# The input loaded and squared in halves of a row block, and two norms' roots made by row block

## The chip, the cores and the metric

The kernel runs on one core of one Trainium2 chip. The metric is the time of one execution on the device in microseconds (us). Three runs of the kernel before gave 892.39, 893.02 and 893.70 us; the median is 893.02 us. In what follows PE is TensorE (the matrix engine), PEld its weight loads, ACT is ScalarE, DVE is VectorE, POOL is GpSimd and SP is SyncE, which here only issues DMA transfers.

## The reference

Two transformer blocks follow each other on 256 rows of 1024 numbers. The first thing that is computed, and what the change touches, is the norm ahead of the first matrix product; the same norm stands ahead of the cross attention:

```python
def rmsnorm(x, g):
    xf = x.astype(jnp.float32)
    y = xf * lax.rsqrt(jnp.mean(xf * xf, axis=-1, keepdims=True) + EPS)
    return (y * g.astype(jnp.float32)).astype(x.dtype)

def first_block(x, mem, ...):
    h = rmsnorm(x, pre_mix_g[l])
    aq, ak, av, hq, hf_fwd, hf_bwd, hi, hg = split_columns(h @ w_in[l], IN_SPLITS)
    ...                                   # self attention and a gated recurrence, joined in `mixed`
    x = x + rmsnorm(mixed, post_mix_g[l])
    h = rmsnorm(x, pre_x_g[l])
    m = rmsnorm(mem, mem_norm_g[l])
    x = x + rmsnorm(memory_cross_attention(h, m, ...), post_x_g[l])
    h = rmsnorm(x, pre_ffn_g[l])
    x = x + rmsnorm(conv_ffn(h, ...), post_ffn_g[l])
```

The second block has the same skeleton: a norm, a large product `h @ w_in`, two kinds of attention, a projection, a norm and a feed-forward net.

## The kernel before

The 256 rows are two row blocks (R = 2) of 128 rows, one row to a partition; `x[:, r, :]` is row block r. Every engine has a program of its own, written out in order, and the engines meet only at semaphores.

**Weights.** SP loads the weights in transfers of mostly 1 MB or less into a ring of four halves. What lies there is cut into pieces of 128x1024 numbers, and each is split in two: ACT writes the rounded high part (`sb_whi`, line 1631), DVE the rest (`sb_wlo`, line 2266), and PE multiplies high by high, high by low and low by high. ACT can only write a high part when the piece that lay in its place has been used by PE, and SP can only load into a half when DVE is done with what lay there. `ahead_of(name, n)` in the program of ACT or DVE marks up to which piece the engine works before it goes on.

**The first norm** (`pre_mix_g`) in the order of its steps:

- SP issues one transfer of 512 KB for each row block of x (line 1473), then the first weight piece (line 1450) and the rest (line 1452).
- ACT squares a whole row block, 128x1024, and the instruction sums along the row (line 1647); a short instruction behind it reads the sum out.
- POOL makes the inverse root from the sum: one TENSOR_SCALAR (mean plus epsilon, line 1501), a wait on its own step, and a power of -0.5 (line 1502).
- DVE multiplies the row block by the root, in two halves of 512 columns (line 2278). It has all four of these ahead of the low part of the first weight piece (line 2266) and that ahead of the low parts of the turned tiles (line 2288).
- PE turns the scaled rows (line 776) into eight tiles of 128 columns by 256 rows. ACT writes the tiles' high parts (line 1662), after the high part of the first weight piece (line 1631); DVE writes their low parts. PE's first product (line 578) needs both.

Ahead of all that PE multiplies zeros (line 766). POOL issues two small transfers behind the second root (lines 1529 and 1531).

**The norm of the cross attention** (`pre_x_g`): ACT squares x in halves of a row block as DVE adds them up (line 1653), four sums in all. POOL waits for all four, adds two and two (line 1511), and makes both row blocks' roots in one go (lines 1501 and 1502). DVE then scales row block 0 (line 2278) and ACT row block 1 (line 1974). PE turns them (line 754) when all four halves are scaled, behind the last product of the fourth part of the memory's weights (`xkv3`). Two of the banks that the turned tiles go to hold that product's results until ACT has copied them out (line 1710).

**`rstd_rows`** (line 1514) is the helper that later norms use: for one row block it takes the first sum as it comes, folds the second in with another TENSOR_SCALAR (lines 1519 and 1521), and makes the root (line 1522).

Of the kernel before, what the change touches and what calls it, by code (L numbers as in the profile page):

```python
# [33 lines left out]
ACT = mybir.ActivationFunctionType  # L34
# [121 lines left out]
def build(nc, a, out):  # L156
    ctx = ExitStack()
    with ctx:
# [132 lines left out]
        for n in GAINS:  # L291
            stats[n] = (stat(R if n in ("pre_mix_g", "mem_norm_g") else 2 * R), stat(R))
        for n in ("w_out", "w_xo", "ffn1", "w_o_2", "ffn2"):
# [49 lines left out]
        def gain_at(name):  # L343
            return COL_GAIN + KT * GAINS.index(name)
# [1095 lines left out]
        def _(sp):  # L1440
# [31 lines left out]
            for r in range(R):  # L1472
                sp.dma_start(x[:, r, :], a["x"][r * P:(r + 1) * P, :]).then_inc(s(f"x_in{r}"), 16)
            load_all(names[:SLOTS])
# [13 lines left out]
        def _(pool):  # L1488
# [37 lines left out]
            for r in range(R):  # L1526
                sums, rstds = (t[:, r:r + 1] for t in stats["pre_mix_g"])
                rstd("pre_mix_g", [(s("pre_mix_g_sq"), r + 1)], sums, D, rstds)
            pool.dma_start(posi[:, :], a["positions_2"].rearrange("(r p) -> p r", p=P),
# [23 lines left out]
            rstd_post("w_out")  # L1553
            rstd_post("pre_x_g")
            for r in range(R):
# [47 lines left out]
        def _(act):  # L1603
# [33 lines left out]
            def pre_norm(name, src, waits, T, gain, between, added=None, before=None):  # L1637
# [5 lines left out]
                for r in range(R):  # L1643
                    if not added:
                        for w in waits[r]:
# [30 lines left out]

            pre_norm("pre_mix_g", x, [[(s(f"x_in{r}"), 16)] for r in range(R)], hT1, gain_at("pre_mix_g"), first_tiles)
            ahead_of("hff", 4)
# [290 lines left out]
            def between_x():  # L1969
                ahead_of("w_xq0", 1)  # L1970
                act.wait_ge(s("pre_x_g_rstd"), 1)
                for c in range(2):
                    q = slice(c * 512, (c + 1) * 512)
                    act.activation(rows[:, 1, q], x[:, 1, q], ACT.Copy, scale=stats["pre_x_g"][1][:, 1:2]
                                   ).then_inc(s("pre_x_g_scaled"), 1)
                ahead_of("w_xq0", 2)
                for r in range(R):
                    take_rows(f"xkv3.{r}", xv[:, r, 512:1024])
# [257 lines left out]
        def _(dve):  # L2236
# [35 lines left out]
            def pre_norm(name, src, T, gain, before, between):  # L2272
                before()
                for r in range(1 if name == "pre_x_g" else R):
                    dve.wait_ge(s(f"{name}_rstd"), r + 1 if name == "pre_mix_g" else 1)
                    for c in range(2):
# [817 lines left out]
```

## Time and profile before

| what | value |
|---|---|
| median of three runs | 893.02 us (892.39 to 893.70) |
| the profiled execution's own time | 893.71 us |
| its span, first to last instruction | 891.9 us |
| PE busy | 880.6 us, 99% of the span |
| DVE busy | 647.9 us, 73% |
| ACT busy | 493.8 us, 55% |
| POOL busy | 92.8 us, 10% |
| DMA, mean over the span | 171 GB/s |
| mean granted PE clock | 0.998 of full speed |

The profiled execution was timed by itself at 893.71 us, 1.8 us more than the span that the profile shows. Busy time says how full an engine was; it doesn't say who waited for whom. For that the page has the chain of work that ended last: 92% of it is PE's.

### The profile page before, as it was taken

The page shows a single profiled execution, that of the slowest core. Times are in us where ns is not written, and L with a number is a line of the kernel's source. Part 1 is how long each engine was busy: PE and PEld are TensorE (multiplying, and loading weights), DVE is VectorE, ACT ScalarE, POOL GpSimd, SP SyncE. Part 2 cuts the span into 40 slices and gives each one's busy share as a digit, 9 for nine tenths or more (in the row PEclk, how much of TensorE's full clock was granted, in tenths as well). Part 3 has the DMA queues.
Part 4 walks back from the last instruction along what each step waited for, and adds up shares of the span by engine and source line. Part 5 has one row for each costly group of instructions (what it writes and reads, how often), then busy time and mean ns, then how long its engine had stood idle before and what let it go on. Part 6 is the DMA issues. An engine that isn't in the chain of part 4 may idle for free.

```text
span 891.9 us, 13262 instructions
## 1 busy us (share of the span) xinstructions
PE 880.6 (99%) x5100; PEld 754.1 (85%) x5100; DVE 647.9 (73%) x1024; ACT 493.8 (55%) x880; POOL 92.8 (10%) x123
## 2 busy tenths in 40 slices
PE   8999999999999999999999999999999999999997
PEld 6988997889889888888789887898888888888886
DVE  5789975574879688789856846677687774766774
ACT  5855665474477465566635366676555772324341
POOL 1324100010010000000133300011031100000000
PEclk9999999999999999999999999999999999999999
DMA  9745423453654455556418644344266554564531
GB/s 314 248 155 177 163 97 131 153 193 115 189 200 154 142 175 185 208 181 245 166 60 283 211 143 142 107 161 170 95 229 195 169 186 142 189 212 165 189 142 48
DMA packets 99502, 152.25 MB, mean 171 GB/s; under 512 B 2608, under 2 KB 66352, under 8 KB 99184
## 3 DMA queue, kind: packets, MB, share of 16 engines
q1 hardware_dynamic: 99040, 150.68, 50.3%
q8 instruction: 41, 0.67, 0.3%
q10 hardware_dynamic: 288, 0.47, 0.2%
q0 software_dynamic: 112, 0.26, 0.1%
q14 instruction: 21, 0.17, 0.1%
HBM read 150.35 MB, written 1.05 MB: 170 GB/s over the span
## 4 chain that ended last, share of the span: by engine, by line
PE 92%; DVE 5%; ACT 2%; issue 1%; DMA 1%; POOL 0%; DVEq 0%; POOLq 0%; SPq 0%; ACTq 0%
PE ps L578 28%; PE ps L571 19%; PE ps L1080 13%; PE ps L636 8%; PE ps L1084 7%; PE ps L668 4%; PE ps L743 2%; PE ps L754 1%; PE ps L831 1%; DVE sb_wlo L2266 1%; PE ps L707 1%; PE ps L1028 1%; PE ps L932 1%; PE ps L1224 1%; ACT sb_whi L1631 1%
## 5 line engine op out<-in xcount | busy, mean ns | idle before, releaser
L2266 DVE TENSOR_TENSOR sb_wlo<-sb_ring,sb_whi 128x1024 fp32r<-128x1024 f32 (+2 forms) x169 | 203.5, 1215 | 81.6 <-ACT sb_whi L1631 81.1
L1631 ACT ACTIVATE sb_whi<-sb_ring 128x1024 fp32r<-128x1024 f32 (+2 forms) x169 | 174.0, 1046 | 101.5 <-PE ps L636 69.5
L578 PE MATMUL ps<-sb_whi,sb_tb 128*128 128x512 f32 (+2 forms) x520 | 128.8, 387 | 0.0
L578 PEld LDWEIGHTS ps<-sb_whi,sb_tb 128*128 128x128 f32 x520 | 93.9, 188 | 17.3 <-issue 1.0
L578 PE MATMUL ps<-sb_whi,sb_ta 128*128 128x512 f32 (+1 forms) x240 | 57.8, 380 | 0.0
L636 PE MATMUL ps<-sb_wlo,sb_tb 128*128 128x512 f32 (+2 forms) x224 | 57.7, 380 | 0.0
L1519 POOL TENSOR_SCALAR sb_st<-sb_st 128x1 f32<-128x1 f32 x14 | 7.3, 524 | 451.6 <-ACT sb_probs L1895 451.6
L2224 ACT ACTIVATE sb_b<-sb_b 128x512 f32<-128x512 f32 x9 | 5.7, 632 | 79.7 <-DVE sb_b L2695 79.7
L578 PEld LDWEIGHTS ps<-sb_whi,sb_ta 128*128 128x128 f32 x240 | 42.3, 188 | 8.6 <-issue 0.5
L636 PEld LDWEIGHTS ps<-sb_wlo,sb_tb 128*128 128x128 f32 x224 | 41.3, 188 | 7.6
L2695 DVE TENSOR_REDUCE sb_b<-ps 128x256 f32<-128x512 f32 x36 | 23.8, 685 | 28.6 <-PE ps L1084 28.6
L1998 ACT ACTIVATE sb_b<-ps 128x256 f32<-128x256 f32 x32 | 12.2, 382 | 52.7 <-PE ps L1084 52.7
L571 PE MATMUL ps<-sb_whi,sb_ta 128*128 128x512 f32 (+1 forms) x120 | 37.5, 377 | 0.1
L578 PE MATMUL ps<-sb_tb,sb_whi 128*128 128x256 f32 x256 | 35.1, 288 | 0.8 <-DVE sb_tb L2288 0.7
L578 PEld LDWEIGHTS ps<-sb_tb,sb_whi 128*128 128x128 f32 x256 | 32.1, 191 | 2.6 <-issue 1.6
L1710 ACT ACTIVATE sb_b<-ps 128x512 f32<-128x512 f32 (+1 forms) x44 | 24.2, 590 | 9.6 <-PE ps L743 4.6
L578 PE MATMUL ps<-sb_ta,sb_whi 128*128 128x256 f32 x192 | 26.5, 290 | 1.4 <-DVE sb_ta L2288 1.4
L2266 DVE TENSOR_TENSOR lent9lo<-sb_ring,lent9hi 128x1024 fp32r<-128x1024 f32 x19 | 23.2, 1220 | 5.9 <-ACT lent9hi L1631 5.9
L2266 DVE TENSOR_TENSOR lent1lo<-sb_ring,lent1hi 128x1024 fp32r<-128x1024 f32 x18 | 22.0, 1221 | 7.5 <-ACT lent1hi L1631 7.5
L2755 DVE SCALAR_TENSOR_TENSOR sb_b<-sb_b,sb_col 128x255 f32<-128x255 f32 x64 | 26.6, 478 | 0.8 <-ACT sb_b L2016 0.8
L578 PEld LDWEIGHTS ps<-sb_ta,sb_whi 128*128 128x128 f32 x192 | 24.8, 197 | 2.0 <-issue 1.6
L571 PEld LDWEIGHTS ps<-sb_whi,sb_ta 128*128 128x128 f32 x120 | 21.9, 188 | 4.7 <-DVE sb_ta L2714 0.5
(430 smaller groups left out, 2068.0 us busy)
## 6 DMA issues: line engine op xcount, KB each, us to landing
sb_ring<-in_w_in SPq DMA_DIRECT2D x32, 1024.0 KB, 5.4
sb_ring<-in_w_up SPq DMA_DIRECT2D x18, 1024.0 KB, 5.1
sb_ring<-in_w_down SPq DMA_DIRECT2D x11, 1024.0 KB, 7.4
sb_ring<-in_w_ffn_down SPq DMA_DIRECT2D x11, 1024.0 KB, 7.5
sb_ring<-in_w_ffn_gate SPq DMA_DIRECT2D x9, 1024.0 KB, 5.3
sb_ring<-in_w_ffn_up SPq DMA_DIRECT2D x9, 1024.0 KB, 5.4
sb_ring<-in_w_xkv SPq DMA_DIRECT2D x8, 1024.0 KB, 5.6
sb_ring<-in_w_out SPq DMA_DIRECT2D x4, 1024.0 KB, 5.1
```

Source lines behind the costliest of these rows:

```text
L571: mm = pe.matmul(o, l[a_], r[b_], start=(start and n == 0), stop=(stop and n == 2), skip_group_check=not check)
L578: pe.matmul(o, l, r, start=(start and n == 0), stop=False, skip_group_check=True)
L636: mm = pe.matmul(o, T[0][:, k0 + i, r * P:(r + 1) * P], w[1][:, i], start=False, stop=k0 + i == k - 1, skip_group_check=True)
L668: mm = pe.matmul(o, T[0][:, k0 + i, r * P:(r + 1) * P], w[1][:, i], start=False, stop=k0 + i == k - 1, skip_group_check=True)
L743: mm = pe.matmul(o, w[1][:, i, :], T[0][:, i, :], start=False, stop=i == KT - 1, skip_group_check=True)
L1080: pe.matmul(o[:, :], w[0][:, k, :], both_halves[f][:, k].rearrange("p two n -> p (two n)"), start=k == 0, stop=False)
L1084: mm = pe.matmul(o[:, 0:S], w[1][:, k, :], T[0][:, k, :], start=False, stop=k == KT - 1)
L1631: act.activation(piece_pair(m)[0], src, ACT.Copy).then_inc(s("hi_done"), 1)
L1710: act.activation(dst, bank[banks.at[key][0]][:, 0:n], ACT.Copy, scale=1.0 if scale is None else scale).then_inc(banks.release(key), 1)
L2266: dve.tensor_tensor(low, pieces[m][1], high.bitcast(F32), ALU.subtract).then_inc(s("lo_done"), 1)
L2695: dve.tensor_reduce(dst[c], o[:, :].rearrange("p (two n) -> p n two", two=2), AX.X, ALU.add).then_inc(banks.release(key), 1)
L2755: dve.scalar_tensor_tensor(dst, src, COL[:, at:at + 1], dst, ALU.mult, ALU.add).then_inc(banks.release(key) if last and c and i < SPLIT_FR ...
```

## The change

The input comes in four transfers of 128x512 in place of two of 128x1024, each with a semaphore of its own. ACT squares it in four halves, each with a sum of its own. Both norms' roots are made by `rstd_rows`, one row block at a time. DVE and ACT wait for the count of the roots that they need: DVE's scaling of row block r waits for root r, and in the cross attention ACT, which scales row block 1, waits for two.

```diff
@@ stats
-            stats[n] = (stat(R if n in ("pre_mix_g", "mem_norm_g") else 2 * R), stat(R))
+            stats[n] = (stat(R if n == "mem_norm_g" else 2 * R), stat(R))
@@ SP
             for r in range(R):
-                sp.dma_start(x[:, r, :], a["x"][r * P:(r + 1) * P, :]).then_inc(s(f"x_in{r}"), 16)
+                for c in range(2):
+                    q = slice(c * 512, (c + 1) * 512)
+                    sp.dma_start(x[:, r, q], a["x"][r * P:(r + 1) * P, q]).then_inc(s(f"x_in{r}{c}"), 16)
@@ POOL
             for r in range(R):
-                sums, rstds = (t[:, r:r + 1] for t in stats["pre_mix_g"])
-                rstd("pre_mix_g", [(s("pre_mix_g_sq"), r + 1)], sums, D, rstds)
+                rstd_rows("pre_mix_g", r)
@@
-            rstd_post("pre_x_g")
+            for r in range(R):
+                rstd_rows("pre_x_g", r)
@@ ACT
                 for r in range(R):
-                    if not added:
+                    if name == "pre_mix_g":
+                        for c in range(2):
+                            act.wait_ge(s(f"x_in{r}{c}"), 16)
+                            q = slice(c * 512, (c + 1) * 512)
+                            act.activation(rows[:, r, q], src[:, r, q], ACT.Square,
+                                           accum_out=stats[name][0][:, 2 * c + r:2 * c + r + 1]
+                                           ).then_inc(s(f"{name}_sq"), 1)
+                    elif not added:
...
-            pre_norm("pre_mix_g", x, [[(s(f"x_in{r}"), 16)] for r in range(R)], hT1, gain_at("pre_mix_g"), first_tiles)
+            pre_norm("pre_mix_g", x, [], hT1, gain_at("pre_mix_g"), first_tiles)
@@
-                act.wait_ge(s("pre_x_g_rstd"), 1)
+                act.wait_ge(s("pre_x_g_rstd"), R)
@@ DVE
-                    dve.wait_ge(s(f"{name}_rstd"), r + 1 if name == "pre_mix_g" else 1)
+                    dve.wait_ge(s(f"{name}_rstd"), 1 if name == "mem_norm_g" else r + 1)
```

POOL at the start of the program, ahead of its first two transfers. `sb_st` holds sums and roots, `sb_neghalf` the power. Before:

```order
L1525 MEMSET sb_neghalf 128x32
L1501 ISA
L1501 TENSOR_SCALAR sb_st<-sb_st 128x1 [waits pre_mix_g_sq,pool_step]
L1502 TENSOR_TENSOR sb_st<-sb_st,sb_neghalf 128x1 [waits pool_step]
L1501 TENSOR_SCALAR sb_st<-sb_st 128x1 [waits pre_mix_g_sq]
L1502 TENSOR_TENSOR sb_st<-sb_st,sb_neghalf 128x1 [waits pool_step]
```

Now:

```order
L1527 MEMSET sb_neghalf 128x32
L1521 ISA
L1521 TENSOR_SCALAR sb_st<-sb_st 128x1 [waits pre_mix_g_sq,pool_step]
L1523 TENSOR_SCALAR sb_st<-sb_st 128x1 [waits pre_mix_g_sq,pool_step]
L1524 TENSOR_TENSOR sb_st<-sb_st,sb_neghalf 128x1 [waits pool_step]
L1521 TENSOR_SCALAR sb_st<-sb_st 128x1 [waits pre_mix_g_sq]
L1523 TENSOR_SCALAR sb_st<-sb_st 128x1 [waits pre_mix_g_sq,pool_step]
L1524 TENSOR_TENSOR sb_st<-sb_st,sb_neghalf 128x1 [waits pool_step]
```

Each row block's root has three instructions in place of two, and the first of them waits only for the first half's sum. The two transfers stand behind six instructions in place of four.

ACT at the start of the program, from its first transfer to the first tile's high part (`sb_ta`). `sb_b` is where the squares go. Before:

```order
L1605 DMA sb_col<-in_ident_col 128x374
L1647 ACT_TABLE_LOAD
L1647 ACTIVATE sb_b0,sb_st<-sb_x 128x1024 [waits x_in0]
L1647 ACTIVATE sb_b0,sb_st<-sb_x 128x1024 [waits x_in1]
L1673 DMA sb_cst<-in_tables 128x544
L1631 ACTIVATE sb_whi<-sb_ring 128x1024 [waits first_piece_in]
L1662 ACTIVATE sb_ta<-ps4,sb_col 128x256 [waits filled4,col_in]
```

Now:

```order
L1607 DMA sb_col<-in_ident_col 128x374
L1650 ACT_TABLE_LOAD
L1650 ACTIVATE sb_b0,sb_st<-sb_x 128x512 [waits x_in00]
L1650 ACTIVATE sb_b0,sb_st<-sb_x 128x512 [waits x_in01]
L1650 ACTIVATE sb_b0,sb_st<-sb_x 128x512 [waits x_in10]
L1650 ACTIVATE sb_b0,sb_st<-sb_x 128x512 [waits x_in11]
L1682 DMA sb_cst<-in_tables 128x544
L1633 ACTIVATE sb_whi<-sb_ring 128x1024 [waits first_piece_in]
L1671 ACTIVATE sb_ta<-ps4,sb_col 128x256 [waits filled4,col_in]
```

Two squares of 128x1024 have become four of 128x512, each with a wait on its own transfer. The high part of the first weight piece still stands behind all squares and ahead of the tiles.

POOL between the norm behind the self attention (`w_out_sq`) and the one ahead of the feed-forward net, in the first block. Before:

```order
L1511 TENSOR_TENSOR sb_st<-sb_st 128x2 [waits w_out_sq]
L1501 TENSOR_SCALAR sb_st<-sb_st 128x2 [waits pool_step]
L1502 TENSOR_TENSOR sb_st<-sb_st,sb_neghalf 128x2 [waits pool_step]
L1511 TENSOR_TENSOR sb_st<-sb_st 128x2 [waits pre_x_g_sq]
L1501 TENSOR_SCALAR sb_st<-sb_st 128x2 [waits pool_step]
L1502 TENSOR_TENSOR sb_st<-sb_st,sb_neghalf 128x2 [waits pool_step]
L1519 TENSOR_SCALAR sb_st<-sb_st 128x1 [waits w_xo_sq]
```

Now:

```order
L1513 TENSOR_TENSOR sb_st<-sb_st 128x2 [waits w_out_sq]
L1503 TENSOR_SCALAR sb_st<-sb_st 128x2 [waits pool_step]
L1504 TENSOR_TENSOR sb_st<-sb_st,sb_neghalf 128x2 [waits pool_step]
L1521 TENSOR_SCALAR sb_st<-sb_st 128x1 [waits pre_x_g_sq]
L1523 TENSOR_SCALAR sb_st<-sb_st 128x1 [waits pre_x_g_sq,pool_step]
L1524 TENSOR_TENSOR sb_st<-sb_st,sb_neghalf 128x1 [waits pool_step]
L1521 TENSOR_SCALAR sb_st<-sb_st 128x1 [waits pre_x_g_sq]
L1523 TENSOR_SCALAR sb_st<-sb_st 128x1 [waits pre_x_g_sq,pool_step]
L1524 TENSOR_TENSOR sb_st<-sb_st,sb_neghalf 128x1 [waits pool_step]
```

In place of one addition, one mean and one power for both row blocks there are two rounds of mean, mean and power, the first of which needs only row block 0.

## Rows read from the trace of the kernel before

**Rows 1.** What PE waited for in the span: in total, times, longest.

```profile
PE ps L578 <- DVE sb_ta L2288: 1.4, 1, 1.4
...
PE ps L578 <- DVE sb_tb L2288: 0.7, 1, 0.7
...
PE ps L754 <- DVE sb_b L2278: 0.2, 1, 0.2
```

**Rows 2.** Timeline of ACT, 0 to 15 us: start, length, what, idle before.

```profile
5.21 1.06 ACT L1647 ACTIVATE sb_b<-sb_x 128x1024 f32<-128x1024 f32 x1 [2.76 <-DMA sb_x<-in_x]
...
6.59 1.06 ACT L1647 ACTIVATE sb_b<-sb_x 128x1024 f32<-128x1024 f32 x1 [0.23 <-DMA sb_x<-in_x]
...
7.55 0.19 ACT L1647 ACTIVATION_READ_ACCUMULATOR sb_b<-sb_x 128x1 f32 x1
8.34 1.06 ACT L1631 ACTIVATE sb_whi<-sb_ring 128x1024 fp32r<-128x1024 f32 x1 [0.60 <-DMA sb_ring<-in_w_in]
```

**Rows 3.** Timeline of POOL, 0 to 12 us.

```profile
6.53 0.19 POOL L1501 TENSOR_SCALAR sb_st<-sb_st 128x1 f32<-128x1 f32 x1 [5.68 <-ACT sb_b L1647]
6.80 0.55 POOL L1502 TENSOR_TENSOR sb_st<-sb_st,sb_neghalf 128x1 f32<-128x1 f32 x1
7.83 0.49 POOL L1501 TENSOR_SCALAR sb_st<-sb_st 128x1 f32<-128x1 f32 x1 [0.47 <-ACT sb_b L1647]
8.40 0.55 POOL L1502 TENSOR_TENSOR sb_st<-sb_st,sb_neghalf 128x1 f32<-128x1 f32 x1
```

**Rows 4.** Timeline of DVE, 0 to 15 us.

```profile
7.39 0.88 DVE L2278 TENSOR_SCALAR sb_b<-sb_x,sb_st 128x512 f32<-128x512 f32 x2 [1.58 <-POOL sb_st L1502]
8.98 1.09 DVE L2278 TENSOR_SCALAR sb_b<-sb_x,sb_st 128x512 f32<-128x512 f32 x2 [0.71 <-POOL sb_st L1502]
9.99 1.21 DVE L2266 TENSOR_TENSOR sb_wlo<-sb_ring,sb_whi 128x1024 fp32r<-128x1024 f32 x1
11.12 3.21 DVE L2288 SCALAR_TENSOR_TENSOR sb_ta<-ps,sb_col,sb_ta 128x256 fp32r<-128x256 f32 x8
```

**Rows 5.** Timeline of PE, 0 to 18 us.

```profile
12.13 3.52 PE L578 MATMUL ps<-sb_ta,sb_whi 128*128 128x256 f32 x16 [1.35 <-DVE sb_ta L2288]
```

**Rows 6.** Timeline of ACT, 181 to 189 us, around the second norm.

```profile
182.98 0.63 ACT L1653 ACTIVATE sb_b<-sb_x 128x512 f32<-128x512 f32 x1
183.51 0.19 ACT L1653 ACTIVATION_READ_ACCUMULATOR sb_b<-sb_x 128x1 f32 x1
...
185.88 1.34 ACT L1974 ACTIVATE sb_b<-sb_x,sb_st 128x512 f32<-128x512 f32 x2 [0.57 <-POOL sb_st L1502]
187.13 1.04 ACT L1631 ACTIVATE sb_whi<-sb_ring 128x1024 fp32r<-128x1024 f32 x1
188.20 1.09 ACT L1710 ACTIVATE sb_b<-ps 128x512 f32<-128x512 f32 x2
```

**Rows 7.** The chain of waits, 165 to 215 us: start, length, what.

```profile
187.71 0.47 PE ps L636 x2
```

**Rows 8.** POOL's second mean of a row block (line 1521), all 14.

```profile
L1521 POOL TENSOR_SCALAR sb_st<-sb_st x14: 264/265/1640, 242.8 to 887.1; 128x1 f32<-128x1 f32 x14
```

**Rows 9.** Timeline of SP, 0 to 16 us: DMA issues, and their length.

```profile
0.73 0.86 SPq L1473 DMA_DIRECT2D sb_x<-in_x  x2
...
2.10 8.02 SPq L1452 DMA_DIRECT2D sb_ring<-in_w_in  x4
```

**Rows 10.** Busy time of engines by stretch, granted clock, DMA share, GB/s.

```profile
4.00:6.50 2.50, 2.50 (x4) 1.01 (x3) 0.41 (x3) 1.15 (x2) 0.00 (x0) 1.00 1.03 380
6.50:8.50 2.00, 1.46 (x8) 0.83 (x7) 0.88 (x2) 1.31 (x3) 1.33 (x4) 1.00 1.19 309
```

**Rows 11.** The same view, of the stretch at the lower clock.

```profile
13.67:17.09 3.42, 3.42 (x16) 3.42 (x17) 2.93 (x4) 1.31 (x2) 0.00 (x0) 0.50 1.08 342
```

**Rows 12.** The chain of waits, 0 to 40 us.

```profile
17.39 1.07 ACT sb_whi L1631
...
35.98 1.60 DVE sb_b L2278 x4
```

## Prediction

> **What bounds the kernel now.** I read four views, in this order. First, what PE waited for. PE is busy for 99% of the span, so a change pays only where PE stands still. Three of its stops lie where this change could touch them: 1.4 us ahead of its first product, 0.2 us ahead of the memory's turned rows, 0.7 us behind the cross attention's norm [rows 1]. Second, the start engine by engine. The first product begins at 12.13 us [rows 5]. Read back from there: DVE's low parts of the tiles from 11.12, its low part of the first weight piece from 9.99, its scaling of row block 1 from 8.98 [rows 4]; POOL's power from 8.40 and mean from 7.83 [rows 3]; ACT's square of row block 1 from 6.59, which had waited for x [rows 2]. Every step begins within 0.1 us of the last one's end, so this chain has no slack. Beside it runs one with little: the first weight piece is there at 8.34 and its high part is done at 9.40 [rows 2], 0.59 us before DVE begins its low part. Third, the second norm: ACT scales row block 1 from 185.88, writes a high part from 187.13, and copies `xkv3` out from 188.20 [rows 6]; PE ends the half of `xkv3` that the copy waits for at 187.71 + 0.47 = 188.18 [rows 7]. So PE sets that start, and the root does not. Fourth, the granted clock: from 13.67 to 17.09 us PE ran at 0.50, its lower level of 1.2 GHz, and at 1.00 around it [rows 11]. It had stood still for 1.35 us ahead of the first product [rows 5]. At 2.4 GHz the 3.42 us of work would have taken 1.71.
>
> **The change part by part.**
>
> *Squares.* Two of 1.06 us become four. For a half I take the second norm's squares: read-out begins 183.51 - 182.98 = 0.53 us after the start and takes 0.19 [rows 6], so the sum is there after 0.72 us, against 7.55 + 0.19 - 6.59 = 1.15 [rows 2]. Only the last half counts: 0.43 us gained if it lands when the row block landed. The first half of each block is squared while the second lands; ACT was idle there (2.76 us).
>
> *Transfers.* The bytes are the same; the source rows are 2 KB long in place of 4 KB, and SP issues two more transfers at 0.86 / 2 = 0.43 us each [rows 9]. So the first weight piece is issued 0.86 us later. From above: the next four issues took 8.02 us [rows 9], 2.0 us each against 0.43, so SP was held up by a full queue and the engines by nothing; the DMA share was already 1.03 [rows 10]. A later issue into a queue that isn't empty costs nothing; at the worst it costs the 0.86 us whole. The Trainium skill speaks for the full queue (DMA: Bandwidth & Descriptors, "Queues, rings and completion order": each engine takes its ring's descriptors in order), so by it the weight piece simply stays behind x. For the shorter rows the trace has no pure case. The nearest are 380 GB/s with x's 4 KB rows and 309 with the weight piece's 512 B rows [rows 10]. 1.05 MB takes 2.76 us at the one and 3.39 at the other: between 0 and 0.63 us later. Rows of 2 KB are nearer to the long ones; I take 0.2 us later for x's halves and for the weight piece. Lower end: the weight piece no longer competes with x, which may land up to 0.2 us earlier.
>
> *POOL.* Row block 0: first half seen early, second half at 5.21 + 0.2 = 5.41, its sum at 6.13. Then a start of 0.09 (as 7.74 to 7.83), a second mean of 0.265 [rows 8], 0.08 to the next, a power of 0.55 [rows 3]: root at 7.11, DVE from 7.15, 0.24 earlier than 7.39. Row block 1: last sum at 6.59 + 0.2 + 0.72 = 7.51. Its two means would begin at 7.17 and 7.60. Here a row speaks against the change: POOL's mean took 0.49 us at 7.83 and 0.19 at 6.53 [rows 3]; the long one began inside DVE's scaling (7.39 to 8.27) and ended 0.05 us behind it [rows 4]. Both means of row block 1 now fall into DVE's scaling of row block 0 (7.15 to 8.03). With the long price: first mean to 7.66, second 7.74 to 8.08, power to 8.71, DVE from 8.74. Without: second mean to 7.87, power to 8.50, DVE from 8.53. I take the first, since the row shows it. The Trainium skill has it as a rule (SBUF — State Buffer, "Who interferes with whom"): whichever of the two takes the shared port pair first holds it for a whole instruction. By that rule the long price stands; without it DVE would be 0.21 us earlier.
>
> *DVE and the first product.* Row block 1 scaled from 8.74 in place of 8.98; its low part of the weight piece could begin 1.01 us later (as 9.99 - 8.98), at 9.75. ACT's high part: 8.34 + 0.2 + 1.06 = 9.60, so the piece is ready. Both chains are now within 0.15 us of each other, which caps what a faster root can bring. The first product moves from 12.13 by 0.24 to 11.89. With x unmoved the root allows 8.55 and the piece 9.56: 0.43 us gained. With everything 0.63 us later: high part at 10.03, low part from 10.18, 0.2 us lost. So the start is worth -0.43 to +0.2 us, and I take -0.3, between the worked 0.24 and the end of 0.43.
>
> *From there to the end.* The 0.2 us wait of PE at 37.6 hangs on a chain of DVE and ACT that begins with ACT's high part at 17.39 and ends in DVE's scaling from 35.98 [rows 12]. That high part waits for PE to be done with the first piece, so both chains move with PE's start, and the gain passes. Cover that doesn't move (a landing) is late nowhere: what DMA must bring by then is queued from 2.10 on.
>
> *POOL's two transfers* now stand behind six instructions, about as early as before: nothing.
>
> *The second norm.* Its root for row block 1 comes after one mean and a power, 0.09 + 0.27 + 0.08 + 0.55 behind the last sum in place of the add, mean and power: up to 0.5 us earlier at ACT's 185.88. ACT waits for PE at 188.20 all the same. Worth 0; at the other end, if POOL is held up by DVE's earlier scaling for over 0.5 us (a second mean has taken up to 1.64 [rows 8]), ACT's high part and its copy begin later and PE pays the rest: 1.64 - 0.27 = 1.37 later, less the 0.5, 0.9 us. At best, if the hand-over at 188.18 isn't PE's after all, the 0.5 us are gained.
>
> **Sum.** 893.71 (the profiled execution: 891.9 of span and 1.8 around it) - 0.3 + 0 = 893.4. That execution is 0.69 us over the median, so the median comes to 893.02 - 0.3 = 892.7 us.
>
> **The rivals.**
>
> *Late x (slower).* SP's two more issues and the short rows put the weight piece and x back by more than 0.45 us; from there DVE's low part begins later than 9.99. For it: the two issues are 0.86 us, more than that. Against it: the full queue. At 0.63 to 0.86 us the start is lost by 0.2 to 0.45: 893.3 on average.
>
> *The clock stays up.* PE's stop ahead of the first product gets shorter, since the turned rows and the product both move, and the stretch at 1.2 GHz doesn't come: 1.71 + 0.3 us less, 891.0. For it: the stretch began 1.5 us after the first product, so little separates the two. Against: the stop of 1.35 us is DVE's and ACT's work on the piece and the tiles, which is not touched.
>
> *The clock stays down longer.* One more stretch of the same length: 892.7 + 1.7 = 894.4. For it: the start now is a different pattern of short bursts. Against: PE has no stop behind 12.13.
>
> *The second norm pays.* 0.5 more: 892.2. Against it is the hand-over from PE at 188.18.
>
> *It doesn't do what it says* would be roots that still come together; the order of POOL excludes it.
>
> **How the numbers follow.** Forecast (its own range 892.4 to 892.9) 0.63; late x 0.15; clock up 0.11; clock longer 0.05; second norm 0.06. No change is what can't be told from it here, 0.2% or 1.8 us either way: 891.2 to 894.8. Forecast, late x and the second norm lie inside, and so does most of the longer clock. Faster by over 0.2%: the clock up, 0.11, and 0.02 for what I have not seen: 0.13. Slower by over 0.2%: the longer clock with late x, 0.04, and 0.02 unseen: 0.06. The same: 0.81. The range takes in the ends of both clock cases: 891.0 to 894.4.
>
> **What would show it right or wrong.** Right: last half of x squared from about 6.8; POOL's means of row block 1 long, 0.3 to 0.5 us, inside DVE's scaling; first product at 11.7 to 11.9; the second norm's copy by ACT still at PE's pace, with PE's wait of 0.7 us there unchanged; all later steps earlier by what the start gained. Wrong: a first weight piece seen after 8.9; a first product after 12.13; PE's stop at 190 gone; a stretch at 0.50 that is missing or twice as long; or any gain that arises behind 190 us, where nothing is changed.

## The result, and the profile after

The change makes the kernel slower: 895.41 us in the median of 15 runs (894.50 to 896.32) against 893.08 (892.39 to 893.81) of the kernel before; ratio 1.0029, interval 1.0022 to 1.0035. That is 0.29%, small but clear of the noise. I had forecast 892.7, with a range of 891.0 to 894.4. The profiled execution took 895.31 us, with a span of 893.5.

Before the two traces are laid side by side, one thing has to be taken out of them. An execution of either kernel may hold a stretch in which PE is granted 0.50 (1.2 GHz), and such an execution is longer. Of the kernel before there are 137 executions beside the experiments. 59 have a mean granted clock of 0.999 or more; they took 892.08 to 892.65 us, median 892.41. The other 78 took 892.10 to 893.78, median 893.16, so the mean clock sorts them well but not cleanly. Of the kernel after, 4 of 15 have 0.999 or more: median 894.65. So at an equal clock the change costs 2.2 us. I give this number ("at the high clock") for the experiments too, with its count.

**The start came out sooner in this execution.** Timeline of ACT after, 0 to 12 us (start, length, what, idle before); it answers to [rows 2].

```profile
4.32 0.63 ACT L1650 ACTIVATE sb_b<-sb_x 128x512 f32<-128x512 f32 x1 [1.87 <-DMA sb_x<-in_x]
...
6.21 0.63 ACT L1650 ACTIVATE sb_b<-sb_x 128x512 f32<-128x512 f32 x1 [0.33 <-DMA sb_x<-in_x]
...
6.88 0.63 ACT L1650 ACTIVATE sb_b<-sb_x 128x512 f32<-128x512 f32 x1
...
7.41 0.19 ACT L1650 ACTIVATION_READ_ACCUMULATOR sb_b<-sb_x 128x1 f32 x1
8.68 1.06 ACT L1633 ACTIVATE sb_whi<-sb_ring 128x1024 fp32r<-128x1024 f32 x1 [1.07 <-DMA sb_ring<-in_w_in]
```

The last half of x is squared from 6.88, 0.29 after the 6.59 at which the whole row block was, and its sum is there at 7.60 in place of 7.74. (ACT didn't wait ahead of it, so the half may have landed sooner.) The first weight piece is seen at 8.68, 0.34 later than 8.34. SP, with the rows that answer to [rows 9]:

```profile
0.73 1.80 SPq L1475 DMA_DIRECT2D sb_x<-in_x  x4
2.57 0.43 SPq L1450 DMA_DIRECT2D sb_ring<-in_w_in  x1
3.05 7.11 SPq L1452 DMA_DIRECT2D sb_ring<-in_w_in  x4
```

POOL and then DVE, as in [rows 3] and [rows 4]:

```profile
6.06 0.27 POOL L1523 TENSOR_SCALAR sb_st<-sb_st 128x1 f32<-128x1 f32 x1 [0.65 <-ACT sb_b L1650]
...
7.04 0.49 POOL L1521 TENSOR_SCALAR sb_st<-sb_st 128x1 f32<-128x1 f32 x1
7.77 0.27 POOL L1523 TENSOR_SCALAR sb_st<-sb_st 128x1 f32<-128x1 f32 x1 [0.25 <-ACT sb_b L1650]
```

```profile
6.99 0.88 DVE L2287 TENSOR_SCALAR sb_b<-sb_x,sb_st 128x512 f32<-128x512 f32 x2 [2.05 <-POOL sb_st L1524]
8.71 1.09 DVE L2287 TENSOR_SCALAR sb_b<-sb_x,sb_st 128x512 f32<-128x512 f32 x2 [0.83 <-POOL sb_st L1524]
9.77 1.23 DVE L2275 TENSOR_TENSOR sb_wlo<-sb_ring,sb_whi 128x1024 fp32r<-128x1024 f32 x1
```

The first product begins at 11.93 (12.13 in [rows 5]). The stretch at 0.50 lies from 12.11 to 15.52, as long as in [rows 11] but 1.57 us earlier; with both, the high part that was at 17.39 in [rows 12] is at 16.64. So this execution leads by 0.75 us there and by 0.66 at 182 us, part of it only by where the stretch lay.

It is one execution. e1, e3 and e4 below have the same start, and e2, e8 and e13 the start of the kernel before up to the roots. The first weight piece was seen at 8.68, 9.19, 9.08 and 8.69 with the new start (the change, e1, e3, e4) and at 8.34, 8.30, 8.28 and 8.20 with the old (before, e2, e8, e13). The first product began at 11.93, 12.45, 12.33 and 11.94 with the new and at 12.13, 12.04 and 11.93 with the old (e8 has another order there). On average the new start is 0.13 us later.

**The second norm gave it back threefold.** Timeline of POOL after, 180 to 189 us:

```profile
181.81 0.53 POOL L1521 TENSOR_SCALAR sb_st<-sb_st 128x1 f32<-128x1 f32 x1 [2.54 <-ACT sb_b L1662]
182.56 1.66 POOL L1523 TENSOR_SCALAR sb_st<-sb_st 128x1 f32<-128x1 f32 x1 [0.22 <-ACT sb_b L1662]
184.30 0.55 POOL L1524 TENSOR_TENSOR sb_st<-sb_st,sb_neghalf 128x1 f32<-128x1 f32 x1
184.94 0.49 POOL L1521 TENSOR_SCALAR sb_st<-sb_st 128x1 f32<-128x1 f32 x1
185.53 1.43 POOL L1523 TENSOR_SCALAR sb_st<-sb_st 128x1 f32<-128x1 f32 x1
187.04 0.55 POOL L1524 TENSOR_TENSOR sb_st<-sb_st,sb_neghalf 128x1 f32<-128x1 f32 x1
```

The kernel before had three instructions there:

```profile
184.44 0.35 POOL L1511 TENSOR_TENSOR sb_st<-sb_st 128x2 f32<-128x2 f32 x1 [4.53 <-ACT sb_b L1653]
184.88 0.19 POOL L1501 TENSOR_SCALAR sb_st<-sb_st 128x2 f32<-128x2 f32 x1
185.16 0.69 POOL L1502 TENSOR_TENSOR sb_st<-sb_st,sb_neghalf 128x2 f32<-128x2 f32 x1
```

Both roots were there at 185.85, 1.48 us behind the last sum (184.18 + 0.19 = 184.37, ACT's last read-out). Now the first is there at 184.85 and the second at 187.59, 3.88 behind the last sum (183.52 + 0.19 = 183.71). In the kernel before, DVE's low part ended at 184.75, 0.04 ahead of the end of POOL's addition, and the mean and the power fell into a gap of DVE:

```profile
183.53 1.22 DVE L2266 TENSOR_TENSOR sb_wlo<-sb_ring,sb_whi 128x1024 fp32r<-128x1024 f32 x1
185.89 0.88 DVE L2278 TENSOR_SCALAR sb_b<-sb_x,sb_st 128x512 f32<-128x512 f32 x2 [1.15 <-POOL sb_st L1502]
```

DVE after had work there (idle only where it waited):

```profile
180.22 2.73 DVE L2617 SCALAR_TENSOR_TENSOR sb_x<-sb_b,sb_st,sb_x 128x512 f32<-128x512 f32 x4
182.87 1.22 DVE L2275 TENSOR_TENSOR sb_wlo<-sb_ring,sb_whi 128x1024 fp32r<-128x1024 f32 x1
184.89 0.88 DVE L2287 TENSOR_SCALAR sb_b<-sb_x,sb_st 128x512 f32<-128x512 f32 x2 [0.80 <-POOL sb_st L1524]
185.68 1.22 DVE L2275 TENSOR_TENSOR sb_wlo<-sb_ring,sb_whi 128x1024 fp32r<-128x1024 f32 x1
```

The mean of 1.66 us began in the last of the four residual steps (to 182.95) and ended at 184.22, 0.13 behind the low part (184.09). The one of 1.43 began in the second half of the scaling (to 185.77) and ended at 186.96, 0.06 behind the next low part (186.90). By these times each waited for the DVE instruction that ran and for the one behind it. The means over the first half's sum (0.53 and 0.49) waited for one.

What followed on ACT answers to [rows 6]:

```profile
187.62 1.34 ACT L1983 ACTIVATE sb_b<-sb_x,sb_st 128x512 f32<-128x512 f32 x2 [2.96 <-POOL sb_st L1524]
188.86 1.05 ACT L1633 ACTIVATE sb_whi<-sb_ring 128x1024 fp32r<-128x1024 f32 x1
189.82 1.05 ACT L1719 ACTIVATE sb_b<-ps 128x512 f32<-128x512 f32 x2
```

And on PE. The kernel before turned all 16 tiles without a stop and began the product at 191.07, after 0.70:

```profile
188.46 1.91 PE L754 MATMUL ps<-sb_col,sb_b 128*128 128x128 f32 x16
191.07 3.00 PE L578 MATMUL ps<-sb_tb,sb_whi 128*128 128x256 f32 x16 [0.70 <-DVE sb_tb L2288]
```

The kernel after:

```profile
189.01 1.09 PE L754 MATMUL ps<-sb_col,sb_b 128*128 128x128 f32 x8 [1.05 <-ACT sb_b L1983]
190.44 1.14 PE L754 MATMUL ps<-sb_col,sb_b 128*128 128x128 f32 x8 [0.34 <-ACT sb_b L1719]
192.66 1.43 PE L578 MATMUL ps<-sb_tb,sb_whi 128*128 128x256 f32 x8 [1.08 <-DVE sb_tb L2297]
```

192.66 - 191.07 = 1.59 later, from a lead of 0.66: 2.25 us lost between 182 and 193, the whole difference at an equal clock; behind 193 nothing more is lost (895.31 - 893.71 = 1.60). The chain of waits after, 175 to 200 us, now goes through POOL:

```profile
182.56 1.66 POOL sb_st L1523
...
185.53 1.44 POOL sb_st L1523
```

### The profile page after: what moved, and what is told of

The parts are those of the page before. It is cut to its first block, busy times and chain, and to the rows that moved or that the text cites. A ratio compares the mean times of both kernels' runs of the same rounds, so it can differ in the third digit from the quotient of the medians.

```text
span 893.5 us, 13277 instructions
## 1 busy us (share of the span) xinstructions
PE 879.8 (98%) x5100; PEld 753.6 (84%) x5100; DVE 648.4 (73%) x1024; ACT 494.9 (55%) x884; POOL 97.4 (11%) x128
## 4 chain that ended last, share of the span: by engine, by line
PE 90%; DVE 5%; ACT 2%; issue 1%; POOL 1%; DMA 1%; SPq 0%; DVEq 0%; POOLq 0%; ACTq 0%
PE ps L578 27%; PE ps L571 19%; PE ps L1080 13%; PE ps L636 7%; PE ps L1084 7%; PE ps L668 4%; PE ps L743 2%; PE ps L754 1%; DVE sb_wlo L2275 1%; PE ps L831 1%; ACT sb_whi L1633 1%; PE ps L707 1%; PE ps L932 1%; PE ps L1028 1%; PE ps L1224 1%
```

## The experiments

Each has 6 to 11 executions. What ran together (e1 to e4, e5 to e8, e9 to e12, e13 to e15, e16 and e17) shares its runs of the kernel before, whose medians lay between 892.49 and 892.64. The ratios are the recorded ones and not quotients of two medians; the two can differ by 0.6 us (e10), so a ratio within 0.0009 of 1 shows no difference. "At the high clock" sets the executions with 0.999 or more against 892.41. Every time inside an execution is from one profiled execution for each experiment.

**e1: the start alone**, the change with the second norm as before.

```diff
-            for r in range(R):
-                rstd_rows("pre_x_g", r)
+            rstd_post("pre_x_g")
...
```

(the waits of DVE and ACT for this norm's roots go back with it)

> The start of the change (transfers and squares in halves, first norm's roots by row block) with the second norm as before. Theory A (the loss is made in the second norm, where POOL's means wait out DVE's instructions on SBUF): the start gains 0.2 us of work and 0.2 to 0.7 with the clock's stretch; median 892.4 to 893.0, and ACT scales row block 1 of the second norm within 1.5 us of the read-out of the last sum again, PE's wait there back at 0.7 us. Rival C (the loss comes from the halves of x at the start, by later weight transfers): about 895.4, like the whole change.

893.74 us (892.04 to 895.57); ratio 1.0009, 1.0000 to 1.0018. At the high clock (4 runs, 892.04 to 893.18) 892.54, 0.1 over before. The median forecast for it, 892.4 to 893.0, was missed. The first product began at 12.45, later than the 11.93 of the change, since the piece was seen at 9.19:

```profile
7.09 0.63 ACT L1649 ACTIVATE sb_b<-sb_x 128x512 f32<-128x512 f32 x1
...
9.19 1.06 ACT L1632 ACTIVATE sb_whi<-sb_ring 128x1024 fp32r<-128x1024 f32 x1 [1.38 <-DMA sb_ring<-in_w_in]
```

So no gain of the start is seen, and its landings scatter; with the second norm as before PE's wait of 0.70 ahead of its product is back.

**e2: the second norm alone**, the kernel before with `rstd_rows("pre_x_g", r)` for each r.

> The kernel before with the second norm's roots made by row block, nothing else. Theory A: PE's first product behind the second norm comes 2.2 us later than before (191.07), at about 193.3; median 895.2 to 895.6. Rival C: 893.1, no change.

895.00 us (894.60 to 895.90, 6 runs); ratio 1.0029, 1.0017 to 1.0040; at the high clock (3) 894.76, 2.3 over. POOL showed the same 1.66 and 1.43 us, and the product began at 192.65 (I had expected 193.3). This part alone is the whole loss.

**e3: DVE waits for both roots**, in the change; ahead of its scaling of row block 0 it now stands idle until the second root too.

```diff
-                    dve.wait_ge(s(f"{name}_rstd"), 1 if name == "mem_norm_g" else r + 1)
+                    dve.wait_ge(s(f"{name}_rstd"), {"mem_norm_g": 1, "pre_x_g": R}.get(name, r + 1))
```

> The whole change, but DVE waits for both roots of the second norm before it scales row block 0, so DVE has nothing to run while POOL makes the second root. Theory A: the second mean of row block 1 falls from 1.43 us to 0.27 and the first from 0.49 to 0.19, that root comes at about 186.1 in place of 187.6, and 0.9 to 1.5 us of the 2.3 come back: median 893.9 to 894.5. Rival B (it is the number of POOL steps, six in a row for three, and their waits on each other): nothing comes back, 895.4.

894.18 us (893.26 to 895.01); ratio 1.0018, 1.0009 to 1.0027; 1.2 under the 895.41 of the change. No execution of it had the high clock. POOL, 182 to 187 us:

```profile
182.94 1.66 POOL L1523 TENSOR_SCALAR sb_st<-sb_st 128x1 f32<-128x1 f32 x1 [0.22 <-ACT sb_b L1662]
184.68 0.55 POOL L1524 TENSOR_TENSOR sb_st<-sb_st,sb_neghalf 128x1 f32<-128x1 f32 x1
185.31 0.19 POOL L1521 TENSOR_SCALAR sb_st<-sb_st 128x1 f32<-128x1 f32 x1
185.61 0.27 POOL L1523 TENSOR_SCALAR sb_st<-sb_st 128x1 f32<-128x1 f32 x1
```

The first mean is as long as ever, since DVE's work there is untouched; the second fell from 1.43 to 0.27 and the one ahead of it from 0.49 to 0.19. POOL has as many steps as in the change, so their number is not what cost this part. Added waiting on DVE made the kernel faster.

**e13: the same with the start as before**, that is e2 with that wait. It was run to have the size without the start's scatter.

> The kernel before with the second norm's roots by row block (two additions, two means, two powers on GpSimd in place of one each), and VectorE waiting for both roots before its scaling. Theory (GpSimd's second mean stands behind VectorE's scaling of row block 0, and the first behind its residual and square work): the first row block's mean stays near 1.66 us, since VectorE still works there, but the second falls from 1.43 to 0.2-0.3 us because VectorE is idle then; the product after it (L578 from sb_tb) starts about 1.0 to 1.3 us before the 192.65 of e2, and the median is 893.2 to 894.2. Rival (the loss is the count of GpSimd's steps and VectorE's later scaling): the second mean stays over 1 us or the scaling's delay makes up for it, and the median is 894.7 to 895.3, as e2's 895.0.

893.22 us (893.01 to 894.45); ratio 1.0006, 0.9997 to 1.0015; at the high clock 893.01 and 893.11, 0.6 over before. So of e2's 2.3 us, 1.7 were the second root standing behind DVE, by five executions; by the two traces, from PE's last products of `xkv3` to the product behind the norm, it is 1.45 of 2.24. The rest is, I think, the first mean's 1.66. My estimate: at 0.27 it would have ended 1.39 sooner, and the round of row block 1 would have found POOL free at its last sum (183.01) in place of 184.24. No run tests it. PE's waits there:

```profile
187.10 2.33 PE L754 MATMUL ps<-sb_col,sb_b 128*128 128x128 f32 x16
190.50 3.00 PE L578 MATMUL ps<-sb_tb,sb_whi 128*128 128x256 f32 x16 [1.07 <-DVE sb_tb L2289]
```

**e4: another form of the sum**, in the change: an addition of the two sums by row block, then one mean, in place of the two means.

```diff
+                pool.wait_ge(s("pre_x_g_sq"), 2 * (r + 1))
+                step(pool.tensor_tensor(m[:, r:r + 1], m[:, r:r + 1], m[:, R + r:R + r + 1], ALU.add))
+                step(pool.tensor_scalar(m[:, r:r + 1], m[:, r:r + 1], 1.0 / D, EPS, ALU.mult, ALU.add))
...
```

> The whole change, but in the second norm each row block's root is made as before the change, by an addition of both sums, a mean with constants and a power, once both sums are there. It asks what it is in the second mean, whose scalar is read from SBUF, that let it wait for two DVE instructions (1.66 and 1.43 us). Theory A1 (an instruction that reads two things from SBUF has to get the port twice): the addition, with two inputs, waits for two as well, about 1.6 us from the same start, and the median is 895 to 895.8. Rival A2 (only the form with a scalar from SBUF does, or it is where it starts): the addition waits for at most one instruction, 0.5 us, the first root comes 1.1 us earlier, the mean behind it waits for at most one, and the median is 893.3 to 894.6.

894.61 us (893.51 to 895.38); ratio 1.0021, 1.0012 to 1.0030. The median lies under the range of A1 and at the edge of A2's.

```profile
182.96 1.68 POOL L1558 TENSOR_TENSOR sb_st<-sb_st 128x1 f32<-128x1 f32 x1 [3.19 <-ACT sb_b L1667]
...
185.51 0.19 POOL L1558 TENSOR_TENSOR sb_st<-sb_st 128x1 f32<-128x1 f32 x1
185.79 0.33 POOL L1559 TENSOR_SCALAR sb_st<-sb_st 128x1 f32<-128x1 f32 x1
186.20 0.67 POOL L1560 TENSOR_TENSOR sb_st<-sb_st,sb_neghalf 128x1 f32<-128x1 f32 x1
```

An addition of two sums at the same place takes 1.68 where the two-sum mean took 1.66. Row block 1's began 0.07 before DVE's scaling and took 0.19. So an addition is held as long as the two-sum mean was, where DVE works, and neither is held where DVE stands idle (0.19 here, 0.27 in e3). The power of 0.67 reads two inputs as well and began inside DVE's scaling, yet didn't wait for the low part behind it (186.38 to 187.60): "two inputs wait for two instructions" is no law by these runs.

**The start: landings.** Seven runs ask what made the piece late. The first three keep the roots as before and square whole blocks.

**e5** has x in the four halves, each with a semaphore, **e11** the four halves with one semaphore for a block, **e6** four transfers of 64 rows of 4 KB. The edit of e11:

```diff
-                sp.dma_start(x[:, r, :], a["x"][r * P:(r + 1) * P, :]).then_inc(s(f"x_in{r}"), 16)
+                for c in range(2):
+                    q = slice(c * 512, (c + 1) * 512)
+                    sp.dma_start(x[:, r, q], a["x"][r * P:(r + 1) * P, q]).then_inc(s(f"x_in{r}"), 16)
...
```

(ACT's wait for a row block is for 32 in place of 16)

> The kernel before with x in four transfers of 128x512, nothing else: the squares stay whole and wait for both halves. Theory D (the halves cost landing time, of x and above all of the first weight piece behind it, which was first used at 8.68 to 9.19 us with them and at 8.30 and 8.34 without): the first weight piece is seen 0.35 to 0.85 us later, PE's first product begins at 12.3 to 12.9 in place of 12.13, and the median is 0.3 to 1.0 us over the kernel before. Rival E (the later landings come from something else, and the halves only lose or gain by the work in between): piece at 8.3, first product at 12.1, no change in the median.

> As the last one, but each transfer carries 64 whole rows of 4 KB in place of 128 half rows of 2 KB: as many transfers and bytes, long rows. Theory D1 (SP's two more issues put the weight piece back by 0.86 us): the same delay as with half rows, piece seen at 8.7 to 9.2. Theory D2 (the short rows are slow): piece seen at 8.3 to 8.5, median as before.

> x in four transfers of 128x512, both halves of a row block on one semaphore and squared whole. It repeats the first of the load experiments without its fault: there the wait on two semaphores stood ahead of ACT's table load, which then cost 1.28 us on the path. Theory D: piece seen at 8.7 to 9.2, x's row block 1 at 6.6 to 7.1, first product at 12.3 to 12.8, median 0.2 to 0.9 over the kernel before, and not the 2.1 of that run.

e5: 894.57 us, ratio 1.0019 (1.0010 to 1.0028). e6: 895.30, 1.0028. Both mislead in one point: with two waits for a block ACT's table load (1.28 us) began behind a landing of x, at 5.25 and 6.29, and the first square came 1.3 us late by it. The landings of the piece stand: 9.09 and 10.30. In e6 its issue was 1.62 later than before and the landing 1.96, with rows as long as before. So a piece can be late without short rows; that short rows cost nothing e6 doesn't show. e11 has no such flaw: 893.19 us, 1.0007 (0.9998 to 1.0016); block 1 squared from 7.59 against 6.59, piece at 9.38, first product at 12.83; at the high clock (4) 892.72, 0.3 over. Halves on one queue bring x itself a microsecond later here, far more than the 0.2 I had taken.

**e10: the issue alone**, two transfers of 4 KB ahead of the weights, x whole.

> The kernel before with two tiny transfers of 128x8 issued by SP between x and the first weight piece; they carry 8 KB and nobody reads them. Only the issue of the weights is 0.86 us later. Theory D1: piece seen at 8.7 to 9.2 in place of 8.34, first product at 12.2 to 12.8, median 0.1 to 0.9 over the kernel before. Rival (a full queue hides a later issue, as the prediction had it): piece at 8.3 to 8.4, no change.

893.06 us (892.25 to 893.59), ratio 1.0000 (0.9991 to 1.0009); at the high clock (4) 892.31. The piece was issued at 2.81 in place of 1.63, 1.18 later, and seen at 8.72, 0.38 later; x was untouched (6.49). So about a third of a later issue reached the landing, though x was still under way when the piece was issued. The first product, at 11.96, didn't feel it.

**e7: two queues.** The change's start, but the right halves of x are issued by ACT, ahead of its table; second norm as before.

```diff
+            for r in range(R):
+                act.dma_start(x[:, r, 512:1024], a["x"][r * P:(r + 1) * P, 512:1024]).then_inc(s(f"x_in{r}1"), 16)
             act.dma_start(ident_col[:, :], a["ident_col"]).then_inc(s("col_in"), 16)
```

> The start of the change with the second norm as before, but the two right halves of x go out from ACT's queue, ahead of its own table transfer, so that SP issues two transfers of x and the weight piece as early as before. Theory D1: piece seen at 8.3 to 8.5 again, DVE scales row block 1 from 8.6 to 8.8, first product at 11.7 to 12.0, median 0.2 to 0.5 us under the kernel before. Theory D2: piece at 8.7 to 9.2 as with the halves from one queue, median 0.5 to 1.2 over it.

892.67 us (892.22 to 894.39), ratio 1.0000; at the high clock (7) 892.37. The squares ran at 4.23, 4.86, 5.78 and 6.41 and the piece was seen at 8.33 as before: the same short halves cost the piece nothing here, where no issue is added to SP's queue (e9 below, with no added issue either, shows that this isn't always so). DVE's lower bounds then waited for the late table and held up the scaling, and the product began at 12.23, later than I had expected.

**e9** (table first, then the right halves) and **e12** (four halves by SP, the weight piece by ACT) look for the better order.

> The two-queue start again, with ACT's own table transfer back in first place and the right halves of x behind it, since the last one found the table late (DVE's first work waited for it until 7.79 and with it both scalings). Second norm as before. Theory D1 (the issue time of the weight piece is what the halves cost): piece seen at 8.3, row block 1 scaled from 8.5 to 8.7, first product at 11.65 to 11.85, median 0.2 to 0.5 us under the kernel before. Rival: the halves from two queues land later than from one (last half after 6.95), and nothing is gained.

> The start of the change with all four halves of x from SP, but the first weight piece issued by ACT, behind its table, at 1.2 us. Second norm as before. Theory D1: the piece is seen before 8.3, as it no longer stands behind x's issues; x, which now shares the engines with it, lands 0.3 to 1.0 us later, and the root decides: first product at 11.9 to 12.5, median within 0.5 us of the kernel before. Rival: the piece is seen at 8.7 or later all the same, because the bytes ahead of it are what counts.

e9: 894.35 us, 1.0017 (1.0008 to 1.0026), squares at 4.15, 6.52, 7.14 and 8.08. e12: 894.72, 1.0020 (1.0011 to 1.0029), squares at 4.32, 5.19, 7.56 and 8.34. First products at 13.24 and 13.39. In both, the later halves of x were squared 1.4 to 1.9 us later than in e7. e9's piece was seen at 8.98; e12's was used at 8.96, right behind the squares, so its landing isn't seen. Why the order of issue does so much isn't shown, and as e7 and e9 ran on different chips, the order may not be all of it. No run of either had the high clock. Windows of e9 (PE, PEld, DVE, ACT and POOL busy, then the granted clock, DMA share, GB/s):

```profile
10.24:17.06 6.82, 5.79 (x26) 5.42 (x27) 6.82 (x13) 4.91 (x10) 1.22 (x2) 0.50 1.09 350
```

Twice as long at 1.2 GHz as in [rows 11]. Ahead of it PE had stood still for 1.51 us before its first turned rows, where it stood for 0.54 in the kernel before.

**e8: the DVE tiles' low parts ahead of the piece's**, in the kernel before.

> The kernel before, but DVE makes the low parts of the turned tiles ahead of the low part of the first weight piece. It asks which step behind the roots holds the first product, since PE needs that low part only after sixteen products. If it is DVE's low part of the piece (1.13 us, with ACT's tiles done beside it from 10.06): first product at 11.7 to 11.8, 0.35 earlier, and a median 0.3 us lower. If the low part is late for PE then (it would be ready at 15.2, PE's sixteen products end at 15.4 at the lower clock): nothing gained, or up to 0.5 us lost in executions where the clock is up.

892.92 us (892.77 to 893.17), ratio 1.0002. The product began at 11.88, but PE waited 0.40 for the piece's low part behind it; at the high clock (6) 892.90, 0.5 over. That is the loss that the expectation had named as its other case.

**e14 and e15: two queues, the table later.** e14 is e7 with DVE's lower bounds behind the first norm and its first low parts, and with PE waiting for the table ahead of its turned rows; e15 has whole blocks, block 1 issued by ACT, roots as before.

```diff
+            pe.wait_ge(s("col_in"), 16)
...
+            pre_norm("pre_mix_g", x, hT1, gain_at("pre_mix_g"), lambda: None, lambda: (ahead_of("hff", 1), dve.wait_ge(s("col_in"), 16)))
+            ahead_of("hff", 4)
             dve.wait_ge(s("col_in"), 16)
...
-            pre_norm("pre_mix_g", x, hT1, gain_at("pre_mix_g"), lambda: None, lambda: ahead_of("hff", 1))
-            ahead_of("hff", 4)
```

> The start as in the change (halves, roots by row block), but the right halves of x issued from ScalarE's queue ahead of the column table, so that the first queue has no added issue; VectorE's preparation of the lower bounds (which waits for that table) stands behind the first norm's scaling and first pieces, and TensorE waits for the table before its transposes. The second norm as before. Theory (what the start lost is issue time in one queue and the table's late landing, not the halves): squares at 4.2 to 6.4 as in e7, VectorE's scaling of row block 1 from about 7.9, first product at 11.2 to 11.7, median 892.0 to 892.4, 0.1 to 0.5 below the kernel before. Rival (the first product is held by the table or the weight's piece and not by the squares): first product at 12.0 to 12.3 and a median of 892.5 to 893.0, as the kernel before.

> The kernel before with whole row blocks, squares and roots as they are, but row block 1 of x issued from ScalarE's queue ahead of the column table, and VectorE's lower bounds moved as in e14. Theory (queue and order decide, halves add little): row block 1 is there 0.3 to 0.6 us sooner than the 6.59 of before, first product at 11.4 to 11.9, median 892.2 to 892.7. Rival (the halves are what brings e7's early squares): row block 1 is squared from 6.5 as before or later, first product at 12.0 or later and median 892.5 to 893.2.

e14: 892.43 us (892.27 to 893.73), ratio 0.9997 (0.9988 to 1.0005); at the high clock (7) 892.35. The product began at 11.61. e15: 893.04, 1.0003 (0.9994 to 1.0012), at the high clock (8) 893.0, 0.6 over; blocks squared from 5.82 and 6.87, product at 12.92. Over two queues the halves brought the product 0.52 sooner than the 12.13 of before, the whole blocks 0.79 later. Yet e14's lead ended 25 us later. PE's turned memory rows in e13 (the start as before, no stretch at 0.50) and in e14:

```profile
36.22 1.97 PE L754 MATMUL ps<-sb_col,sb_b 128*128 128x128 f32 x16 [0.17 <-DVE sb_b L2279]
```

```profile
36.25 1.97 PE L754 MATMUL ps<-sb_col,sb_b 128*128 128x128 f32 x16 [0.53 <-DVE sb_b L2287]
```

0.32 us ahead at the first product (11.93 and 11.61), level there. In between DVE had the lower bounds, moved to 17.90 in front of the angle tables, 0.35 us of work.

**e16 and e17** move these three instructions behind the tables, e17 the mask's cast too.

> As e14 (halves of x over two queues, first norm's roots by row block, second norm as before), but VectorE's preparation of the lower bounds, three instructions that stood from 17.90 to 18.25 ahead of the angle tables, stands behind them, where VectorE waits 1.42 us for ScalarE. Theory (the start's lead was given back because these stand in the chain to the memory's norm): the angle tables are done 0.3 us sooner, TensorE's wait at its turned memory rows falls from 0.53 to about 0.2, that step begins at 35.9 in place of 36.25, and the median is 892.0 to 892.2. Rival (another chain, a landing or ScalarE's table loads, sets that step): it stays at 36.2 and the median at 892.3 to 892.6.

> As e16, with the mask's cast (0.29 us, at 18.25 in e14) behind the angle tables too. Theory (the same chain, still bound by VectorE): another 0.2 us, TensorE's wait at its turned memory rows 0.0 to 0.1, the step at about 35.75, and the median 891.8 to 892.1. Rival (past e16 TensorE itself is the bound, or the positions' landing): the step begins no sooner than in e16 and the median is that of e16 within 0.1 us.

e16: 892.12 us (891.87 to 893.28), ratio 0.9996 (0.9988 to 1.0005); at the high clock (4) 892.10.

```profile
35.95 1.97 PE L754 MATMUL ps<-sb_col,sb_b 128*128 128x128 f32 x16 [0.18 <-DVE sb_b L2287]
```

e17: 891.91 us (891.79 to 893.05), ratio 0.9990, 0.9981 to 0.9999; at the high clock (5) 891.88. It beats the kernel before by 0.5 us at an equal clock, though its ratio is barely clear of 1, and is the best version found. Each step gave about what the chain said: 0.25 and 0.22 us. In e17's trace PE no longer waits at its turned memory rows.

## Why the prediction was wrong

*The second norm* is the step that failed. I put it at "Worth 0", with 0.9 us at the other end: it was 2.3 (e2). I had seen that POOL might be "held up by DVE's earlier scaling", and had the price, "1.37 later", nearly right (1.43 - 0.27 = 1.16 measured). Three things were missed. The mean of row block 0 was held too, behind DVE's residual steps and low part: 1.66 us, where I had given no thought to the round of row block 0. Row block 1's round therefore started at 184.94, 1.23 us behind the last sum, when in the kernel before the shared addition began 0.07 behind its own. That also took away the 0.5 I had taken off, the time by which an undisturbed root would come earlier. And there was no cushion. "So PE sets that start, and the root does not" was true by 0.01 us: ACT's scaling and high part ended at 187.13 + 1.04 = 188.17, PE's half at 188.18 ([rows 6, 7]). The root came 187.59 - 185.85 = 1.74 later, which against PE's lead of 0.66 is 2.40, and PE's product 2.25 later. e2, e3 and e13 show it: this part alone loses 2.3, and with DVE idle the second mean is short and 1.7 of the 2.3 us are back.

The Trainium skill has the lock that I used at the start (SBUF — State Buffer, "Who interferes with whom"): a DVE instruction with two SBUF inputs contends with a GpSimd one that reads SBUF. The residual step (`sb_b`, `sb_x`) and the low part are such, and the trace agrees that they contend, with 1.66 us. How long, it doesn't settle: a hold of one DVE instruction, as I reckoned at the start, is at most the low part's 1.22, and both long means waited out two. Looked up for every step of this norm, as it was for the first, the rule would have named the place of the loss, though not its whole size.

*Transfers.* "A later issue into a queue that isn't empty costs nothing" was wrong: 1.18 us later at issue were 0.38 at the landing (e10, one execution; four with the old issue times scatter by 0.14). In the change it was 0.94 and 0.34, more than the 0.2 taken but inside the range of 0 to 0.63. e1's 9.19, e3's 9.08 and e11's 9.38 lay outside it, with the piece issued at 2.58, 2.56 and 2.56 like the 2.57 of the change; what makes landings of halves scatter stays open.

*Squares, POOL and DVE at the start* went as worked out: DVE at 8.71 (8.74 forecast), the long mean of 0.49 inside the scaling and the second one of 0.27, the product at 11.93 (11.89). But that was partly luck: of four executions with this start e1's and e3's had 12.45 and 12.33. Over the runs the start's "- 0.3" was +0.1 at the high clock, and the four traces give the same 0.1. In the median e1 lost more. It may be that fewer executions hold the high clock (4 of 11, and 4 of 15 of the change; 59 of 137 of before), but those are too few to tell.

*From there to the end* the gain passes in the change, whose wait at the turned memory rows stayed at 0.2. e14 shows how thin that was: 0.35 us of DVE's work ahead of the angle tables, and it didn't.

*The rivals.* Late x did happen in part. The clock's stretch was put at 1.7 us. The kernel before pays up to 1.4 for it (892.41 against up to 893.78); that waits for other engines hide the rest is argued, not shown. So the 891.0 of the rival in which the clock stays up was out of reach: the kernel before takes 892.41 with the clock up, and the start gained nothing. No rival held the loss; those on the slower side were in the wrong place, and POOL "held up by DVE's earlier scaling" was only a clause of the sum.

## What to carry to other kernels

Splitting one small shared step into rounds, each as its inputs come, can move it from a place where its neighbour was nearly idle to where the neighbour works. Look up, for every instruction of each round, what the engine that shares its access to memory is doing then. Where an added step ends in a row of instructions with no gap before the bounding engine's next start, it has no slack, however idle the engine looks above it. And follow a gain at the start through every later meeting of the engines: e14's 0.32 us died behind three instructions of no weight of their own.

## What had not been expected of the hardware

- A POOL mean over 128x1 numbers, 0.27 us by itself, took 1.66 and 1.43 us beside DVE: it waited for two DVE instructions, the second of which began after it. Means over the first sum alone waited for one (0.53, 0.49). Why two, and why the power of 0.67 in e4 did not wait for the low part behind it, these runs don't settle.
- With x in four transfers of the same bytes, the first was seen at 6.29 when it held 64 whole rows (e6) and at 5.25 when it held 128 half rows (e5); a whole block of twice the bytes was seen at 5.21 in the kernel before. One execution each.
- Where ACT had two waits ahead of its first square, its table load of 1.28 us began only when x landed, at 5.25 and 6.29 (e5, e6); with a single wait it began at 1.17 and 1.16 (before, e11), far ahead of the landing.
